# Sums of the weighted modulation rows: products with a column of ones instead of transposes and a VectorE reduction

## What is computed

```python
s_lat = jax.nn.silu(c)[:, None, :]
s_ctx = jax.nn.silu(c_ctx)[None, None, :]
for i in range(DEPTH):
    mod_l = jnp.split(s_lat @ ada_w[i] + ada_b[i], ADA_CHUNKS, axis=-1)
    mod_c = jnp.split(s_ctx @ ada_w[i] + ada_b[i], ADA_CHUNKS, axis=-1)
    h_lat = modulate(x_lat, mod_l[0], mod_l[1])
```

## Time and profile before

| | |
|---|---|
| time, median of 3 runs | 2119.3 us (2115.14 to 2119.72) |
| time of the profiled execution | 2119.23 us |
| its span | 2117.4 us |
| mean granted PE clock | 0.984 |
| PE busy, instructions | 95%, 11090 |
| DVE busy, instructions | 63%, 1640 |
| ACT busy, instructions | 40%, 993 |
| POOL busy | 3% |

### The profile page before, as it was taken

The page is one execution under the profiler, slowest core; times in us unless marked ns, Lnnn a source line. Parts: engine busy times, 40 slices in busy tenths (PEclk is TensorE's granted clock), DMA queues, the critical chain, the costliest instruction groups (busy, mean ns, idle before and its releaser), DMA issues.

```text
span 2117.4 us, 27084 instructions
## 1 busy us (share of the span) xinstructions
PE 2012.3 (95%) x11090; PEld 1705.8 (81%) x11090; DVE 1332.5 (63%) x1640; ACT 849.8 (40%) x993; POOL 68.4 (3%) x121
## 2 busy tenths in 40 slices
PE   5999999998999999889888999999999999999998
PEld 3778777777888888667767998889799978988997
DVE  3877869465666354485566545667765566767555
ACT  4332322232322122245565443555444435645442
POOL 0000000010111000000000000000000000000000
PEclk9999999999999999999998999999999999999999
DMA  9543344242454343233124664555465545446652
GB/s 330 179 143 124 135 147 143 88 159 70 139 159 159 105 135 120 74 101 109 50 83 136 181 196 142 193 181 169 160 219 185 193 145 184 166 152 218 198 180 79
DMA packets 250733, 319.28 MB, mean 151 GB/s; under 512 B 10097, under 2 KB 166034, under 8 KB 250098
## 3 DMA queue, kind: packets, MB, share of 16 engines
q1 hardware_dynamic: 234880, 262.24, 38.7%
q0 software_dynamic: 14416, 53.14, 7.7%
q10 hardware_dynamic: 1314, 2.18, 0.3%
HBM read 316.47 MB, written 1.05 MB: 150 GB/s over the span
## 4 chain that ended last, share of the span: by engine, by line
PE 72%; DVE 14%; DVEq 6%; ACT 3%; DMA 2%; ACTq 2%; issue 1%; SPq 0%
PE ps L2180 22%; PE ps L2182 22%; PE ps L2181 22%; DVE w_lo L1226 3%; PE ps L2197 3%; DVE raw L1341 2%; DVEq L1336 2%; DMA raw<-ret_w_in 1%; PE ps L2353 1%; ACT w_hi L595 1%; ACTq L604 1%; DVEq L1243 1%; DVEq L1239 1%; ACT arena L847 1%; DMA raw<-ada_w 1%
## 5 line engine op out<-in xcount | busy, mean ns | idle before, releaser
L1226 DVE TENSOR_TENSOR w_lo<-raw,w_hi 128x2048 fp32r<-128x2048 f32 (+1 forms) x244 | 553.0, 2272 | 314.9 <-ACT w_hi L595 313.9
L595 ACT ACTIVATE w_hi<-raw 128x2048 fp32r<-128x2048 f32 (+1 forms) x244 | 461.7, 1896 | 266.7 <-PE ps L2182 250.1
L2180 PE MATMUL ps<-h_hi,w_hi 128*128 128x256 f32 x1120 | 320.0, 286 | 2.9 <-DVE h_lo L1231 2.9
L2181 PE MATMUL ps<-h_lo,w_hi 128*128 128x256 f32 x1120 | 318.1, 284 | 0.0
L2182 PE MATMUL ps<-h_hi,w_lo 128*128 128x256 f32 x1120 | 318.0, 284 | 0.0
L2180 PE MATMUL ps<-w_hi,big_hi 128*128 128x512 f32 x760 | 299.8, 394 | 5.5 <-DVE w_lo L1226 3.7
L2181 PE MATMUL ps<-w_lo,big_hi 128*128 128x512 f32 x760 | 296.5, 390 | 0.0
L2182 PE MATMUL ps<-w_hi,big_lo 128*128 128x512 f32 x760 | 296.5, 390 | 0.0
L2180 PEld LDWEIGHTS ps<-h_hi,w_hi 128*128 128x128 f32 x1120 | 216.1, 193 | 5.5 <-issue 4.4
L2181 PEld LDWEIGHTS ps<-h_lo,w_hi 128*128 128x128 f32 x1120 | 216.1, 193 | 0.8 <-issue 0.2
L2182 PEld LDWEIGHTS ps<-h_hi,w_lo 128*128 128x128 f32 x1120 | 216.1, 193 | 0.0
(11 more groups left out here) (289 smaller groups left out, 2638.1 us busy)
## 6 DMA issues: line engine op xcount, KB each, us to landing
raw<-ffn_w_in SPq DMA_DIRECT2D x88, 512.0 KB, 5.2
raw<-w_in SPq DMA_DIRECT2D x80, 512.0 KB, 4.6
raw<-w_up SPq DMA_DIRECT2D x64, 512.0 KB, 4.8
raw<-w_down SPq DMA_DIRECT2D x64, 512.0 KB, 4.6
raw<-ret_w_in SPq DMA_DIRECT2D x48, 512.0 KB, 5.6
front<-ada_w POOLq DMA_DIRECT2D x24, 1024.0 KB, 5.5
raw<-ffn_w_out SPq DMA_DIRECT2D x40, 512.0 KB, 4.6
raw<-ada_w POOLq DMA_DIRECT2D x64, 256.0 KB, 3.3
```

The costliest lines, as they stand in the source:

```text
L595: act.activation(SPLIT_HI[PAIR_OF[u]][:, 0:m], raw[:, RAW_OF[u], 0:m], ACT.Copy).then_inc(sem["hi_ready"], 1)
L1226: op(SPLIT_LO[PAIR_OF[u]][:, 0:m], raw[:, RAW_OF[u], 0:m], SPLIT_HI[PAIR_OF[u]][:, 0:m].bitcast(F32), ALU.subtract).then_inc(sem["lo_ready ...
L2180: pe.matmul(out, a[0], b[0], start=start, stop=False)
L2181: pe.matmul(out, a[0], b[1], start=False, stop=False)
```

## The change

`extra` makes eight products in place of eight transposes: a block of `acc` is stationary, as before, and the moving operand is one column of ones. Each gives 128 sums in one PSUM column; all eight columns stand side by side in bank b, in the order in which `mod` keeps them. DVE's reduction and its drain go, and the bias is added straight from PSUM. PE waits once more, for `ones_set`, which POOL sets at the start of the kernel.

```diff
@@ mod_sums, DVE @@
                 m = mod[:, d, 4 * n:4 * n + 4, :]
-                dve.tensor_reduce(m.rearrange("p j m -> p m j"), ps[:, b:b + 2, :].rearrange("p m (j n) -> p m j n", j=4), AX.X, ALU.add)
-                drain()
-                op(m, m, bias, ALU.add).then_inc(sem["mod_ready"], 1)
+                op(m, bank(b)[:, 0:8].rearrange("p (j m) -> p j m", m=2), bias, ALU.add).then_inc(sem["mod_ready"], 1)
@@ extra, PE @@
                 pe.wait_ge(sem["ada_used"], done)
-                for m in range(2):
-                    for j in range(4):
-                        i = turn(bank(b + m)[:, j * P:(j + 1) * P], acc[:, m, j * P:(j + 1) * P])
+                pe.wait_ge(sem["ones_set"], 1)
+                for j in range(4):
+                    for m in range(2):
+                        i = pe.matmul(bank(b)[:, 2 * j + m:2 * j + m + 1], acc[:, m, j * P:(j + 1) * P], ones[:, 0:1], start=True, stop=True)
                 i.then_inc(sem["at_full"], 1)
```

## The result

The changed kernel takes 2128.74 us (median of 4 runs, 2128.31 to 2130.1) against 2118.42 us for the one before (4 runs): a ratio of 1.0052, 95% interval 1.0035 to 1.0070. A second set, beside nine runs of before, gave 2130.44 and 1.0059 (1.0047 to 1.0072). So it is slower, by 10.3 us in the first set and 12.6 in the second. The forecast was 2131 (range 2124 to 2138), 11.7 more than before.

The account below looks back on a forecast made before the run. PE was taken to bound the kernel (busy 95% of the span). Longer groups cost 17.4 us, less 4.6, 0.4 and 0.7 of ended waits: +11.7 on 2119.23, said as 2131 us, range 2124 to 2138.

Parts of the forecast that it names:

- Two records a product: PE's groups: a float32 product leaves two load-and-matmul records, a transpose one, so 320 instead of 160.
- 0.11 us a pair, set by the load: PE's groups: 16 pairs at 0.11 make 1.76 us, 0.87 more a group, 17.4 us over 20 groups.
- Four stalls, 4.6 us: PE's wait before each head's third group ends because DVE loses the reductions ahead of the last weigh: 4.6 us gained.
- only widens DVE's lead: Third group of a head: PE's later start, after two longer groups, was given no gain of its own.
- The rival in which the stalls stay: Third groups held by ACT or a transfer, not the reductions, so only the cost arrives: 2136.7 us, chance 0.07.
- 0.67 before `gate_rows` and 0.4 at `mod_read`: PE's waits for DVE's additions go: 0.67 us before gate_rows, four times 0.1 at mod_read behind third groups.
- The last group's wait stays: PE's 9.30 us wait before the last group stays, since no reduction stands ahead of that last weigh piece.
- The size: Whole kernel: 11.7 us slower, 2131 us, the forecast case given chance 0.70.
- The clock as a rival: PE's clock falls in a third of the groups, 14 us on top, 2145 or in all 2171; chance 0.07.
- the loads would keep the array at work: PE's groups: argument against a clock fall, though a group of 1.8 us hardly streams columns.

Follow-up runs that it names:

- one_pass2: Changed kernel with accumulators and ones in the rounded fp32r format, two equal columns of ones, one record a product: 2112.82 us, 0.9979 of the kernel before.
- wide128: Changed kernel with 128 moving columns of ones in place of one: 2129.78 us, 1.0056 of the kernel before.
- dve_only: Kernel before with its transposes but without DVE's reduction (sum over the rows left out): 2111.2 us, 0.9970 of the kernel before.
- pe_only: Changed kernel with DVE's reduction and drain put back into a scratch column: 2129.41 us, 1.0063 of the kernel before.
- sums_later: Kernel before, transposes and reductions kept, each head's second reduction moved behind the weigh that the third group waits for: 2116.2 us, 0.9998 of the kernel before.
- sums_placed: Kernel before, reductions kept but moved: second and third behind each head's last weigh, ahead of vb's split; o2's ahead of o4's split: 2112.38 us, 0.9974.

## Why the prediction was right

- **Two records a product.** Counting the records against the code gave 320 instead of 160. This step decided the sign. 320 stand there, and `one_pass2`, with one each, gives the cost back.
- **0.11 us a pair, set by the load.** Measured 1.795 us a group, 0.112 a pair; forecast 1.76, so the term was 18.2 and not 17.4 us at the full clock. I had taken 0.11 where the row of line 2565 gave 0.112. That the load sets it is shown by `wide128` and by the two kernels with fewer stationary columns. My reading that some 107 ns of a load are the passage of its 128 columns, at 0.83 ns each, is right: the steady pitches of 0.1117, 0.0583 and 0.0317 us differ by just that, with 5 ns a pair on top, which I had not seen.
- **Four stalls, 4.6 us.** They went, for 4.65, and DVE's relief is enough for that (`dve_only`). But I gave them to the relief alone and said of PE's later start that it "only widens DVE's lead". That later start clears them by itself, all but 0.1 us each, and the 0.4 at `mod_read` with them (`pe_only`). The sum came out since a stall can go only once, whoever removes it; that this step left the number whole is luck. As gains and losses of independent worth, relief and cost put the kernel without the relief at 2136, and it took 2129.4. The rival in which the stalls stay (2136.7) had no ground for the same reason: with groups this long they could not have stayed.
- **0.67 before `gate_rows` and 0.4 at `mod_read`.** Both went in the changed kernel: the first as forecast; PE comes to the second without a gap. That the first came from the reduction is shown by place: the wait of 0.51 is there in `pe_only` and `sums_later`, whose reduction stands at this place as before, and gone in `dve_only` and `sums_placed`. The four times 0.1 at `mod_read` are gone in those two as well, but also in `pe_only`: either cause is enough.
- **The last group's wait stays.** It did: 9.33 us against 9.30. What I had not priced is that this group runs at the lower clock, where 16 pairs take 3.41 us and not 1.8: 0.9 us more than I had counted for it.
- **The group at 563 us.** Its wait of 0.47 (0.65 with the tail) is no work of the reductions: DVE waits 3.99 us for a piece that POOL's transfer brings at 554.8 us, and from there works almost without a pause until 562.9. It went in the kernels in which PE is later (`pe_only` and `wide128` too) and stayed in `dve_only`, with 0.38. I had not named it among the waits.
- **The size.** 2131 against 2128.7 and 2130.4. Up to the last group it was 13.1 us in one profile and 11.9 in the other against the 11.7 of the sum, and I let the sum run on to the end of the span unchanged, where the waits and the clock behind the changed code took 2.9 and 0.8 of it. That these errors have opposite signs is luck.
- **The clock as a rival** got 0.07, and did not happen in the heads with groups of this length. With groups twice as long it did, and cost 40 us.

## What to carry to other kernels

Before a transpose is traded for a product, count what each leaves on PE: here a float32 transpose is one load and one matmul, and a float32 product two of each, and with up to 128 moving columns the loads are the whole price. Work taken off an engine that is not the bottleneck is worth the waits that it ends, no more; look first whether a change in that engine's order ends them too, and clear the next wait along with the first, since a stall that is cleared at one semaphore reappears at the one behind it. And gains and costs that meet at the same wait don't add.

## What the runs showed of the hardware that I had not expected

- 32 pairs of load and matmul with one moving column (3.6 us), without any wait, brought PE's clock from 2.4 to 1.2 GHz in or behind 9 of the 11 groups in the heads; the same pairs with 128 moving columns never did in the heads. The Trainium skill ("TensorE: Matmul & The Clock Gate", Part 1) says that the clock follows "how busy the PE has been recently"; the trace shows PE busy for the same 385.5 us of 390 in both kernels, and the clock at 0.94 and at 1.00. The busy time that the profile lists does not tell the two kernels apart, and I had argued from it that the loads would keep the array at work.
- One-column and 128-column moving operands cost the same where each product loads a new full block: 1.70 us for 16 pairs.
- At the lower clock a pair with 128 stationary columns costs twice as much too: 16 pairs in 3.41 us, 0.213 each.
- With one moving column the steady pitch of load and matmul was 0.83 ns a stationary column plus 5 ns at 2.4 GHz (0.1117, 0.0583 and 0.0317 us for 128, 64 and 32) and 1.67 ns a column at 1.2 GHz (0.2133, 0.1067 and 0.0533).
